# A hybrid Hyena, attention and expert trunk: where TensorE runs the long convolution's first forward transform

## The reference

```python
def hyena_branch(p_hy, sc_w, sc_b, flt, flt_bias):
    u = short_conv(p_hy, sc_w, sc_b)
    v, x1, x2 = jnp.split(u, 3, axis=-1)
    h_freq = hyena_filters(L, *flt)
    z = v
    for o, gate in enumerate((x1, x2)):
        z = gate * (long_conv(z, h_freq[:, o]) + flt_bias[o] * z)
    return z
```

## Time and profile before

| | |
|---|---|
| median of 3 executions | 2646.34 us |
| lowest, highest | 2644.46, 2648.69 us |
| the profiled execution | 2645.14 us |
| its span, first to last instruction | 2643.4 us |
| mean granted TensorE clock | 0.982 |
| layer 0: Hyena product's stage ends, convolution's begins | at 326.2 us |
| layer 1: the same | at 1639.0 us |

### The profile page before, as it was taken

The page is one execution under the profiler, slowest core; times in us unless marked ns, Lnnn a source line. Parts: engine busy times, 40 slices in busy tenths (PEclk is TensorE's granted clock), DMA queues, the critical chain, the costliest instruction groups (busy, mean ns, idle before and its releaser), DMA issues. The chain is left out here.

```text
span 2643.4 us, 35473 instructions
## 1 busy us (share of the span) xinstructions
PE 2419.1 (92%) x13020; PEld 1518.6 (57%) x13020; DVE 1073.5 (41%) x2144; ACT 622.0 (24%) x1374; POOL 690.8 (26%) x644
## 2 busy tenths in 40 slices
PE   7999988999999999998888899989999999988887
PEld 3455665455555565555555468645787665555553
DVE  5764477444222563211111175844432732222222
ACT  4441122443110232221111142234211311111111
POOL 0003132565321012222221222246431022222221
PEclk9999999999999999999999899999999999999999
DMA  9982030020212639999999913012135699999996
GB/s 360 363 344 101 15 108 19 13 55 19 53 48 88 238 124 389 393 399 402 401 390 388 347 52 119 32 32 55 47 74 196 241 355 395 391 407 403 403 404 240
DMA packets 191103, 588.27 MB, mean 223 GB/s; under 512 B 47425, under 2 KB 109164, under 8 KB 134669
## 3 DMA queue, kind: packets, MB, share of 16 engines
q1 hardware_dynamic: 166485, 551.86, 55.4%
q0 software_dynamic: 22400, 29.42, 3.4%
q10 hardware_dynamic: 2103, 5.51, 0.5%
HBM read 581.31 MB, written 51.51 MB: 239 GB/s over the span
## 5 line engine op out<-in xcount | busy, mean ns | idle before, releaser
L2643 PE MATMUL ps<-w,moe_xt 128*64 128x256 f32 x2816 | 338.2, 394 | 65.4 <-DMA w<-in_w_up_e 63.0
L2783 POOL DMA_INDIRECT rows_out<-moe_rows_out,table x128 | 118.6, 926 | 739.2 <-DVE moe_rows_out L2848 372.5
L2643 PEld LDWEIGHTS ps<-w,moe_xt 128*64 128x64 f32 x2816 | 219.6, 141 | 153.5 <-issue 72.3
L2898 DVE TENSOR_TENSOR moe_gated<-ps,moe_gated 64x256 f32<-64x256 f32 x128 | 54.5, 426 | 502.0 <-ACT moe_gated L2867 501.9
L2867 ACT ACTIVATE moe_gated<-ps 64x256 f32<-64x256 f32 x128 | 48.2, 377 | 667.9 <-PE ps L2643 667.9
L2643 PE MATMUL ps<-early_w,moe_xt 128*64 128x256 f32 x1280 | 152.0, 391 | 29.8 <-DMA early_w<-in_w_up_e 29.7
L1692 POOL TENSOR_SCALAR attn_p<-attn_p,attn_rs 128x768 f32<-128x768 f32 (+1 forms) x80 | 155.4, 1950 | 81.2 <-DVE attn_rs L1866 80.7
L2651 PE MATMUL ps<-w,moe_ht 128*64 128x512 f32 x704 | 170.4, 604 | 2.3 <-issue 2.3
L2164 PE MATMUL ps<-w_out,mix 128*128 128x512 f32 x320 | 144.6, 602 | 7.0 <-PEq L150 7.0
L2884 DVE TENSOR_TENSOR moe_rows_out<-ps,moe_row_gate 64x512 f32<-64x512 f32 x128 | 88.1, 688 | 138.6 <-PE ps L2651 136.6
L2643 PEld LDWEIGHTS ps<-early_w,moe_xt 128*64 128x64 f32 x1280 | 101.0, 140 | 66.9 <-issue 31.9
(11 more groups left out here) (431 smaller groups left out, 4274.1 us busy)
## 6 DMA issues: line engine op xcount, KB each, us to landing
w<-in_w_gate_e SPq DMA_DIRECT2D x88, 1024.0 KB, 25.5
w<-in_w_up_e SPq DMA_DIRECT2D x88, 1024.0 KB, 29.6
w<-in_w_down_e SPq DMA_DIRECT2D x88, 1024.0 KB, 29.5
prep_w<-in_w_ada SPq DMA_DIRECT2D x24, 2048.0 KB, 15.7
early_w<-in_w_gate_e SPq DMA_DIRECT2D x40, 1024.0 KB, 25.1
early_w<-in_w_up_e SPq DMA_DIRECT2D x40, 1024.0 KB, 29.6
early_w<-in_w_down_e SPq DMA_DIRECT2D x40, 1024.0 KB, 29.7
w_merge<-in_w_in SPq DMA_DIRECT2D x32, 512.0 KB, 5.4
```

The lines of the kernel that those rows point to most:

```text
L2643: last = nc.tensor.matmul(ps[k * SLOTS:(k + 1) * SLOTS, 0:DE], xt[:, c], wgu[:, k, c], start=c == 0, stop=c == KC - 1)
L2783: nc.gpsimd.indirect_dma_start(out=dram["y"], out_offset=bass.IndirectOffsetOnAxis(ap=m.table[0:SLOTS, j:j + 1], axis=0), in_=y[:, j % 2], ...
L2898: nc.vector.tensor_tensor(h[:, b % 2], m.ps[SLOTS:2 * SLOTS, b % 2, 0:DE], sg[SLOTS:2 * SLOTS, b % 2], ALU.mult).then_inc(s["h_done"], 1)
```

## The change

`hyena_in_stage` is given `dft0` and its semaphore. At the end of PE's program there the 16 identity products go; in their place PE waits for the load of the matrices, for the last evacuation of v, and for DVE's last reads of banks 0 to 3, and runs the forward transform of job 0 (stream 0, first half of the channels) into those banks, where the next stage looks for it. In `conv_stage`, forward 0 is one increment of its semaphore.

```diff
@@ hyena_in_stage, PE
-            keep_warm(nc, m, 4, 16)
+            dft, dft_in = dft0
+            pe.wait_ge(dft_in, 16)
+            pe.wait_ge(s["tr_evac"], 2 * HC)
+            pe.wait_ge(s["u3_done"], NP)
+            pe.wait_ge(s["u2_done"], NP)
+            pe.wait_ge(s["c22_done"], NP)
+            pe.wait_ge(s["c21_done"], NP)
+            long_forward(nc, m, dft, m.v, 0, 0)
@@
+def long_forward(nc, m, dft, src, tok0, half):
+
+    cols = slice(half * (HW // 2), (half + 1) * (HW // 2))
+    for e, residue in enumerate(FORWARD):
+        last = nc.tensor.matmul(m.ps[:, e // 2, (e % 2) * (HW // 2):(e % 2 + 1) * (HW // 2)], dft[:, e], src[:, tok0 + residue, cols],
+                                start=True, stop=True)
+    return last
@@ conv_stage, PE
             def forward(i):
+                if i == 0:
+                    pe.sem_inc(s["fwd_done"], 1)
+                    return
@@
                 if t == 0:
-                    for e, residue in enumerate(FORWARD):
-                        last = nc.tensor.matmul(m.ps[:, e // 2, (e % 2) * HALF:(e % 2 + 1) * HALF], dft[:, e], src[:, tok0 + residue, cols],
-                                                start=True, stop=True)
-                    last.then_inc(s["fwd_done"], 1)
+                    long_forward(nc, m, dft, src, tok0, half).then_inc(s["fwd_done"], 1)
                     return
```

More of the change, by code:

```diff
@@ L1012, in hyena_in_loads, with hyena_in_stage @@
     return run
-def hyena_in_stage(nc, m, l, w_in, streams, early, then):
+def hyena_in_stage(nc, m, l, w_in, streams, early, dft0, then):
     n_tok = sum(n for _, _, n in streams)
@@ L2535, in conv_loads @@
                     conv_load(sp, conv_early, name, l, 0, consts, dram)
-            hyena_in_stage(nc, m, l, a["w_in"], streams, hyena_early, conv_loads)
+            hyena_in_stage(nc, m, l, a["w_in"], streams, hyena_early, conv_early["dft0"], conv_loads)
             until_conv.close()
```

## The result

The changed kernel takes 2653.28 us in the median of 10 executions (2648.84 to 2659.62), the kernel before 2647.96 in as many runs (2644.35 to 2649.48). The ratio is 1.0029, with a 95% interval of 1.0018 to 1.0041: 7.7 us slower, 4.8 to 10.9; the two medians by themselves are 5.3 us apart, inside that interval. The forecast of no measurable difference does not hold; the change is a small loss.

The account below looks back on a forecast made before the run. Around each layer's barrier, DVE's chain and that of w_qkv's load, latent 0, forward 1 and copy bound unfold 1. +1.70 and +2.41 gave +4.11 us: 2649.25 against the profiled 2645.14, median 2650.4, range 2645.5 to 2654.0.

Parts of the forecast that it names:

- The forecast of no measurable difference: Whole kernel: median 2650.4 us, +0.16%, under the 0.2% a measurement can tell; within 0.2% given 0.60.
- the case of a gain: At unfold 1: w_qkv's load not the later chain, both layers keep their head start; −6.3 us, 2640.0; 9%.
- The transform in the old stage: End of the Hyena stage: layer 0's barrier stays, covered by DVE with 0.65 us; layer 1's comes 0.72 us later.
- The head start is worth only the slack: At unfold 1: DVE, 3.5 and 2.8 us earlier, waits for forward 1's copy; gains only 0.21 and 0.22 us.
- The clock falls in the pause: PE idle 6.43 us (layer 0) and 5.77 us (layer 1) before latent 0; work restarts at the lower clock.
- Its price, 1.91 us: Latent 0 and forward 1 after PE's pause: 1.91 us lost per layer to low clock, bounds 1.42 and 2.98.
- From here everything moves as a whole.: Behind unfold 1: all later work shifts together by the delays there, +1.70 us in layer 0, +2.41 in layer 1.
- the low clock lasts longer: PE's restart in both layers: at least 2.5 us lost per layer, +5.3 to +7.5 us in all; 24%.
- the forecast's own range: Sum over both layers at unfold 1: +3.1 to +5.3 us; 55%.

Follow-up runs that it names:

- after_warm: The changed kernel plus 22 identity products on PE behind the barrier, where it waits for w_qkv; ratio to the kernel before 1.0006.
- only_layer1: The change made in layer 1 alone, layer 0 left as in the kernel before; ratio to the kernel before 1.0017, 4.5 us slower.
- only_layer0: The change made in layer 0 alone, layer 1 left as in the kernel before; ratio to the kernel before 1.0015, 4.0 us slower.
- before_warm_inv: The kernel before plus 8 identity products in PE's pauses ahead of the first two inverse transforms of each layer; ratio to the kernel before 1.0015.
- after_swap: The changed kernel with latent 0 behind forward 1 in the order, no identity products added; ratio to the kernel before 1.0013.
- after_swap_warm: The changed kernel with latent 0 behind forward 1, and 14 identity products between barrier and forward 1; ratio to the kernel before 1.0002.
- after_swap3: As after_swap_warm, with latent 0's root ahead of GpSimd's first sine sum and ACT keeping latent 0 before normalising latent 1; 2643.53 us, ratio 0.9982.

## Why the prediction was wrong

The change was called a loss of 4.1 us that could hardly be told from none (0.16%); it is 7.7 us by the ratio, 5.3 by the medians, and clear of none, with an interval of 0.12% to either side. That 2653.28 lies inside the range given, 2645.5 to 2654.0, supports nothing: the range took in all but the case of a gain. Point by point, as it was put:

- *The transform in the old stage.* Right: layer 0's barrier did not move, layer 1's moved by 0.73 us (4.51 for 3.78), forecast 0.72.
- *The head start is worth only the slack.* Right: unfold 0 came 3.6 and 2.9 us earlier, and unfold 1 waits 5.2 us for the copy of forward 1, behind latent 0 and its load. Filling the pause gives a at −0.3 and +0.4 us, forecast −0.2 and +0.5.
- *The clock falls in the pause.* Right, in 8 of 8 places, and shown by after_warm.
- *Its price, 1.91 us.* **This term was too small**: 2.35 in the mean, 1.8 to 2.7. I took the mean of three restarts, of which two followed short pauses (2.30 us at 349.09, which I did not even name, and 3.37 at 1721.64), through which the granted clock stayed at 1.00 and fell only as work came back. Through the 4.08 us ahead of 409.24 it is 0.79, as it is through the 6.43 us here (0.79): that restart, with 2.42 lost, was the one to go by. With it the sum at unfold 1 is 5.1; the four profiles give 4.8.
- *"From here everything moves as a whole."* **This is the step that failed.** It took the low stretches of the kernel before as part of the path to be moved. The one at the first inverse transform was hidden under DVE and kept the pause ahead of the second one short. In the changed kernel the fall comes one transform later, where DVE waits: 1.7 to 2.3 us more in b of layer 0 in each of four profiles. The sum had no term for it. That the change as such moves the fall there is not shown: only_layer1 has it in a layer 0 as before.
- *The case "the low clock lasts longer".* It ran from 5.3 to 7.5 us in all and had 24%. The outcome is at its upper end, 7.7, but by other means: 2.35 per restart, where the case begins at 2.5, and the second transform for the rest. At unfold 1 alone the 4.8 us lie in the forecast's own range, 3.1 to 5.3. The case is not borne out by its number.

About 1 us of the measured difference lies in neither stretch. It may lie behind them: in layer 1 the stretch from the attention's first product to the experts' first (L2659 in the kernel before) varies from 385.7 to 391.1 us over the profiles and is 386.7 in the mean of three before, 388.3 in the mean of four changed, but one of the three (388.8) is as long as the changed ones, so no cause is shown. The microsecond is within the interval.

## What to carry to other kernels

Work pulled ahead of a barrier is only worth what its consumer can use. Ask which other chain meets it next and how far apart the two are; here it was 0.2 us. Then ask what the moved work had been covering on its own engine: here the transform and the identity products together kept PE's pauses at 1.8 us, and without them a pause of 6 us sent the clock down just ahead of the path's work. To collect part of the head start, the order of the consumers had to change with it, on PE, ACT and GpSimd.

## What the runs showed of the hardware

- Executions of one kernel can agree closely in where the clock falls. In three of three profiles of the kernel before it falls as PE comes back for layer 0's first inverse transform, with b at 110.7 to 110.8 us; in four of four of the changed kernel it falls at the second. But the length of the pause does not decide it: behind the same 2.30 us that transform takes 5.38 in the kernel before and 3.69 in only_layer1, whose layer 0 was not edited. The Trainium skill's page "TensorE: Matmul & The Clock Gate", section "Part 1: The HAM clock gate", describes a rhythm that runs freely, and in the four profiles of the change the loss at the restart does vary, from 2.0 to 2.7 us in layer 0; but a fall that is at the same place in three of three and four of four is not what I had taken from it.
- A longer pause does not cost in proportion. Pauses of 5.7 to 6.9 us cost 1.8 to 2.7, one of 7.75 (only_layer0) 3.0, one of 2.81 (before_warm_inv) already 1.7, and one of 3.22, ahead of latent 2 in layer 1, nothing in after_swap (16 records in 3.69 us, granted clock 1.00) and 2.2 in after_swap_warm (5.92).
- The first product on w_qkv starts between 5.4 and 6.9 us behind the load's issue over the kernels in which PE waits for it, though nothing about the load was edited.
- DVE's sum at L1563 took 3.06 us in the last timeline above, with GpSimd's sine sum (338.56 to 340.90) running beside it; the same sum takes 1.27 at 356.22, where GpSimd's has all but ended. The longer one ends 1.09 us behind GpSimd's, as if most of it had been held up until then; that is read from one pair of rows, and no run tests it. It is some 1.8 us of DVE's time that after_swap3 spends there.
